# Dense down's weight sums on VectorE, and the experts' up and gate products wide then narrow over two quarters at a time

## The reference, cut to what matters

```python
def _swiglu(h, w_gate, w_up, w_down):
    return (jax.nn.silu(h @ w_gate) * (h @ w_up)) @ w_down

def _moe(h, w_router, w_gate, w_up, w_down):
    """Top-2-of-8 SwiGLU experts, softmax over the selected logits, sorted grouped dispatch."""
    ...
    logits = jnp.einsum('td,de->te', xf, w_router, preferred_element_type=F32)
    top_logits, top_idx = lax.top_k(logits, TOP_K)
    gates = jax.nn.softmax(top_logits, axis=-1)
    ...
    hid = jax.nn.silu(lax.ragged_dot(xs, w_gate, group_sizes)) * lax.ragged_dot(xs, w_up, group_sizes)
    ys = lax.ragged_dot(hid, w_down, group_sizes)
    ys = ys * gates.reshape(-1)[order][:, None].astype(ys.dtype)
    out = jnp.zeros_like(xf).at[tok_sorted].add(ys)
    return out.reshape(B, S, D)

def second_block(x, ...):
    ...
    for l in range(DEPTH_2):
        h = _rmsnorm(x, mix_norm[l])
        ...
        x = x + jnp.concatenate([a, r], axis=-1) @ w_out[l]
        h = _rmsnorm(x, ffn_norm[l])
        if l % 2 == 0:
            x = x + _swiglu(h, dense_w_gate[j], dense_w_up[j], dense_w_down[j])
        else:
            x = x + _moe(h, moe_router[j], moe_w_gate[j], moe_w_up[j], moe_w_down[j])
    return _rmsnorm(x, final_norm)
```

## Time and profile before

| what | us |
|---|---|
| median of three runs | 1756.85 (1754.42 to 1758.68) |
| the profiled execution, time | 1754.76 |
| its span in the trace | 1753.0 |
| TensorE busy | 1699.0 (97%) |
| VectorE, ScalarE, POOL busy | 506.8, 298.9, 290.7 |
| dense stage, column blocks and down | about 500 to 733 in the trace |
| experts | about 898 to 1746 |

### The profile page before, as it was taken

How to read it: one execution, slowest core, us unless ns; L and a number is a source line. 1 busy time by engine, 2 the same in 40 slices (tenths; PEclk the granted TensorE clock), 3 DMA queues, 4 the chain that set the end, 5 groups by cost and what they waited for, 6 DMA issues and landing times.

```text
span 1753.0 us, 25352 instructions
## 1 busy us (share of the span) xinstructions
PE 1699.0 (97%) x11012; PEld 830.0 (47%) x11012; DVE 506.8 (29%) x870; ACT 298.9 (17%) x592; POOL 290.7 (17%) x207
## 2 busy tenths in 40 slices
PE   8999999999999998999999999999999999999997
PEld 4586664455644453447544433343443334444332
DVE  3643224243654236366341100110110101102012
ACT  1210222134311010134211111020110201102011
POOL 0210000042457867037000000000000000000000
PEclk9999999999999998999999999999999999999999
DMA  9742116644334353444648999999999999999997
GB/s 328 262 145 98 49 73 183 225 147 145 104 137 151 115 210 112 159 158 148 238 159 350 422 418 426 420 424 421 390 418 419 426 421 420 422 398 389 421 420 293
DMA packets 114017, 484.84 MB, mean 277 GB/s; under 512 B 15828, under 2 KB 24421, under 8 KB 89966
## 3 DMA queue, kind: packets, MB, share of 16 engines
q1 hardware_dynamic: 106544, 466.53, 67.3%
q0 software_dynamic: 3056, 10.88, 1.7%
q10 hardware_dynamic: 4302, 5.75, 1.0%
HBM read 477.08 MB, written 8.15 MB: 277 GB/s over the span
## 4 chain that ended last, share of the span: by engine, by line
PE 86%; DMA 8%; DVE 2%; issue 2%; ACT 1%; SPq 0%; POOL 0%; ACTq 0%; DVEq 0%; POOLq 0%
PE bank L3299 22%; PE bank L1299 18%; PE bank L1311 14%; PE bank L3363 7%; PE bank L3315 7%; PE bank L3373 4%; DMA ring<-in_moe_w_up 3%; DMA ring<-in_moe_w_down 2%; PE bank L550 2%; PE bank L625 2%; PE bank L1322 2%; PE bank L3331 2%; DMA shift_rows<-ring 1%; DMA ring<-shift_rows 1%; PE bank L1931 1%
## 5 line engine op out<-in xcount | busy, mean ns | idle before, releaser
L3299 PE MATMUL bank<-ring,work 128*64 128x512 f32 x1400 | 397.5, 601 | 8.1 <-DMA ring<-in_moe_w_up 7.3
L1299 PE MATMUL bank<-ring,work 128*128 128x512 f32 (+3 forms) x944 | 387.9, 566 | 5.9 <-DVE work L2303 2.8
L1299 PEld LDWEIGHTS bank<-ring,work 128*128 128x128 f32 x944 | 174.1, 191 | 194.3 <-issue 172.2
L3299 PEld LDWEIGHTS bank<-ring,work 128*64 128x64 f32 x1400 | 124.7, 138 | 206.4 <-issue 204.7
L1311 PE MATMUL bank<-ring,work 128*128 128x512 f32 (+1 forms) x458 | 196.5, 583 | 10.5 <-issue 10.5
L3299 PE MATMUL bank<-work 128*64 128x512 f32 x392 | 172.7, 594 | 0.0
L3363 PE MATMUL bank<-ring,work 128*64 128x512 f32 x704 | 156.8, 595 | 4.3 <-DMA ring<-in_moe_w_down 4.3
L1311 PEld LDWEIGHTS bank<-ring,work 128*128 128x128 f32 x458 | 87.3, 192 | 111.0 <-issue 109.4
L3463 POOL DMA_DIRECT2D expert_rows<-work x7 | 3.6, 521 | 764.5 <-DVE work L3526 605.2
L3315 PE MATMUL bank<-ring,work 128*32 128x256 f32 x1736 | 125.4, 380 | 0.0
L3363 PEld LDWEIGHTS bank<-ring,work 128*64 128x64 f32 x704 | 49.6, 137 | 100.5 <-issue 99.5
(11 more groups left out here) (474 smaller groups left out, 1774.9 us busy)
## 6 DMA issues: line engine op xcount, KB each, us to landing
ring<-in_moe_w_down SPq DMA_DIRECT2D x43, 2048.0 KB, 18.3
ring<-in_moe_w_gate SPq DMA_DIRECT2D x26, 2048.0 KB, 20.2
ring<-in_moe_w_up SPq DMA_DIRECT2D x24, 2048.0 KB, 18.6
ring<-in_w_in SPq DMA_DIRECT2D x20, 2048.0 KB, 8.7
ring<-in_moe_w_up SPq DMA_DIRECT2D x25, 1536.0 KB, 10.9
ring<-in_moe_w_gate SPq DMA_DIRECT2D x23, 1536.0 KB, 13.5
work<-in_moe_w_down SPq DMA_DIRECT2D x12, 2048.0 KB, 16.2
work<-in_moe_w_up SPq DMA_DIRECT2D x8, 2048.0 KB, 22.2
```

Source lines behind the costliest of these rows:

```text
L1299: mm = pe.matmul(banks(j)[:, 0:width], x[:, k0 + kt, tt * P:(tt + 1) * P], w[:, kt, c0:c0 + width], start=first and n == 0, stop=last and ...
L3299: mm = pe.matmul(out[rows, :], xgT[:, q * tiles + k, 0:64], w[n][:, k, cols], start=(q == 0 and k == 0), stop=last)
```

## The change

In the dense stage the down product's weight sums of part 0 stay on POOL; those of parts 1 to 5 are issued by VectorE, each after the part's row sums. `turned_last` comes after part 1's weight sums. On TensorE, product `one` no longer waits for the row sums; product `three` does.

In the experts the quarters are taken in groups of two. Before a group TensorE waits for all of its loads (four), and gives all four slots back at its end. The order in a part becomes wide 0, wide 1, narrow 0, narrow 1 | narrow 2, narrow 3, wide 2, wide 3. In the very first part (e = 0) the groups are (0), (1), (2, 3), and the last runs wide, wide, narrow, narrow. Turns follow each of the two wide quarters of part 1; the wide pick comes after the first group, the narrow pick between narrow 3 and wide 2.

```diff
--- before.py
+++ after.py
@@ -2573,6 +2573,26 @@
         w = core.view(chunk)
         return [w[:, tiles, cols] for tiles in (slice(0, n), slice(n, 2 * n)) for cols in (slice(0, BANK), slice(BANK, DM))]
 
+    def sum_weights(eng, i):
+        chunk, _, n = parts[i]
+        b11, b12, b21, b22 = down_blocks(i)
+        one, two, four = (t[:, 0:n, :] for t in down_weights[i])
+        summed = 4 * n_cols + 4 * i
+        core.wait_weights(eng, chunk)
+        eng.wait_ge(*sevens.weights_summed.at(summed))
+        if i < 4:
+            eng.wait_ge(*banks.ready(J["first", n_cols - 2 + i // 2]))
+        else:
+            eng.wait_ge(down_done, i - 3)
+        eng.tensor_tensor(one, b12, b11, ALU.subtract).then_inc(sevens.weights_summed.sem, 1)
+        eng.wait_ge(*sevens.weights_summed.at(summed + 1))
+        eng.tensor_tensor(two, b22, one, ALU.subtract).then_inc(sevens.weights_summed.sem, 1)
+        eng.wait_ge(*sevens.weights_summed.at(summed + 2))
+        eng.tensor_tensor(b12, b22, b12, ALU.subtract).then_inc(sevens.weights_summed.sem, 1)
+        eng.wait_ge(*sevens.weights_summed.at(summed + 3))
+        eng.tensor_tensor(four, b21, two, ALU.subtract).then_inc(sevens.weights_summed.sem, 1)
+        eng.wait_ge(*sevens.weights_summed.at(summed + 4))
+
     @core.block.tensor
     def _(pe):
         def weights(c):
@@ -2645,10 +2665,9 @@
                                        five=(r1, one, 1), six=(r2, two, 2), seven=(r3, t3, 4))[name]
             if name == "one":
                 core.wait_weights(pe, chunk)
+            elif name == "three":
                 pe.wait_ge(*sevens.rows_summed.at(4 + i + 1))
-                if i == 0:
-                    banks.enter(pe, J[name])
-            elif i == 0:
+            if i == 0:
                 banks.enter(pe, J[name])
             if summed:
                 pe.wait_ge(*sevens.weights_summed.at(4 * n_cols + 4 * i + summed))
@@ -2748,23 +2767,7 @@
             pool.wait_ge(*sevens.weights_summed.at(4 * c + 3))
             pool.tensor_tensor(four, gate[:, hi, :], two, ALU.subtract).then_inc(sevens.weights_summed.sem, 1)
             pool.wait_ge(*sevens.weights_summed.at(4 * c + 4))
-        for i, (chunk, _, n) in enumerate(parts):
-            b11, b12, b21, b22 = down_blocks(i)
-            one, two, four = (t[:, 0:n, :] for t in down_weights[i])
-            summed = 4 * n_cols + 4 * i
-            core.wait_weights(pool, chunk)
-            if i < 4:
-                pool.wait_ge(*banks.ready(J["first", n_cols - 2 + i // 2]))
-            else:
-                pool.wait_ge(down_done, i - 3)
-            pool.tensor_tensor(one, b12, b11, ALU.subtract).then_inc(sevens.weights_summed.sem, 1)
-            pool.wait_ge(*sevens.weights_summed.at(summed + 1))
-            pool.tensor_tensor(two, b22, one, ALU.subtract).then_inc(sevens.weights_summed.sem, 1)
-            pool.wait_ge(*sevens.weights_summed.at(summed + 2))
-            pool.tensor_tensor(b12, b22, b12, ALU.subtract).then_inc(sevens.weights_summed.sem, 1)
-            pool.wait_ge(*sevens.weights_summed.at(summed + 3))
-            pool.tensor_tensor(four, b21, two, ALU.subtract).then_inc(sevens.weights_summed.sem, 1)
-            pool.wait_ge(*sevens.weights_summed.at(summed + 4))
+        sum_weights(pool, 0)
 
     @core.block.vector
     def _(dve):
@@ -2853,11 +2856,11 @@
             if c:
                 turned(c - 1)
         for i in range(len(parts)):
-            if i == split:
-                sum_rows(i)
+            sum_rows(i)
+            if i:
+                sum_weights(dve, i)
+            if i + 1 == split:
                 turned_last()
-            else:
-                sum_rows(i)
         for tt in range(NT):
             dve.wait_ge(*lead.rows[tt])
         j, got = done("one")
@@ -3259,32 +3262,36 @@
             chunks = range(PARTS[n][0], sum(PARTS[n]))
             if n == 0:
                 pe.wait_ge(xg_ready, e + 1)
-            for q in range(QUARTERS):
-                i = 2 * (QUARTERS * n + q)
-                landed(e, i)
-                landed(e, i + 1)
-                w = [first_view(core, e, i), first_view(core, e, i + 1)]
-                if e + n + q == 0:
+            groups = [(0,), (1,), (2, 3)] if e + n == 0 else [(0, 1), (2, 3)]
+            for g, qs in enumerate(groups):
+                w = {}
+                for q in qs:
+                    i = 2 * (QUARTERS * n + q)
+                    landed(e, i)
+                    landed(e, i + 1)
+                    w[q] = [first_view(core, e, i), first_view(core, e, i + 1)]
+                if e + n + g == 0:
                     for k, forms in enumerate(((part_wide, part_narrow), (part_narrow, part_wide))):
                         for form in forms:
                             for c in chunks:
-                                form(e, c, w, q, (c - chunks[0]) * BANK, (k,))
+                                form(e, c, w[q], q, (c - chunks[0]) * BANK, (k,))
                         if k == 0:
                             halves_left[0] = 1
                     pending[0] += 2
                     continue
-                for m, form in enumerate((part_wide, part_narrow)[::-1 if q % 2 else 1]):
-                    for c in chunks:
-                        if form is part_wide or NARROW[e]:
-                            form(e, c, w, q, (c - chunks[0]) * BANK)
-                    if n and q < 2 and m == 0:
-                        turn_chunk(e, 2 * q)
-                        turn_chunk(e, 2 * q + 1)
-                pending[0] += 2
-                if n and q == 1 and e + 1 < NE:
+                for m, form in enumerate((part_wide, part_narrow)[::-1 if g % 2 else 1]):
+                    for q in qs:
+                        for c in chunks:
+                            if form is part_wide or NARROW[e]:
+                                form(e, c, w[q], q, (c - chunks[0]) * BANK)
+                        if n and g == 0 and m == 0:
+                            turn_chunk(e, 2 * q)
+                            turn_chunk(e, 2 * q + 1)
+                    if n and g and m == 0 and e + 1 < NE:
+                        pick_narrow(e + 1)
+                pending[0] += 2 * len(qs)
+                if n and g == 0 and e + 1 < NE:
                     pick(e + 1)
-                if n and q == 2 and e + 1 < NE:
-                    pick_narrow(e + 1)
 
         def part_wide(e, c, w, q, first, ks=range(KD // QUARTERS)):
             out, cols, tiles = wide_of(c), slice(first, first + BANK), KD // QUARTERS
```

## The result

| | before | after |
|---|---|---|
| median, us | 1755.63 (1753.63 to 1758.68, 4 runs) | 1811.13 (1808.23 to 1815.77, 4 runs) |
| the profiled execution | 1754.76 | 1808.23 |
| its span | 1753.0 | 1806.4 |
| experts' first matmul to the first matmul of the scatter | 897.84 to 1742.05 | 894.46 to 1795.49 |

A forecast was written before the change was run, and what follows sets the result against it. The expert stage was taken as a stream of loads that TensorE keeps up with. Dense down -2.2 and experts +50.6 on 1754.76 gave 1803.2 us, forecast as 1804; own range 1795 to 1812, eight in ten 1790 to 1813.

The forecast's parts named there:

- Dense down, -2.2: Dense down: the 10.53 us wait goes, VectorE's added sums bring a new 8.3 us wait before product six; -2.2 us.
- The bound of -13: Dense down: the gain if VectorE were never late with its sums, 10.5 + 2.5 us.
- End of part 0 in e = 0, +3.1: Experts, e = 0: block 4 waits for the first wide multiplication, late after narrow matmuls; +3.1 us (0 to 5).
- The start of e = 2: Experts: e = 2 starts 9.0 (later slots) + 10.0 (four loads before the first matmul) later, and by the 3.1.
- The start of e = 5: Experts: e = 5 starts another 9.0 + 10.0 us later, its stream paced by load (3, 17).
- The ledger: Experts: delays from slots given back later and from waiting for four loads, added up at e = 2, e = 5 and the end.
- The end, +9.0: End of experts: the last load of e = 7, paced by (6, 17), comes 9.0 us later, with no four-load cost.
- The clock, +1.5: Waits before e = 2 and e = 5: slow matmuls cost 3.0 us each, against 1.5 and 3.0 before; +1.5.
- Nine slots did not hold: Experts, rival 1: two groups of four fit in nine slots, every load lands in time; 1751.6 us, chance 0.04.
- Half of it: Experts, rival 2: queued loads cover the later slots, only the fourth load counts, twice; 1776 us, chance 0.1.
- VectorE's sums did not fall to POOL's pace: Dense down, rival 3: VectorE's sums run at POOL's pace, +14 in place of -2.2; 1819 us, chance 0.05.
- The groups formed: Experts, rival 4 said they don't: waits or give-backs still go by single quarters; about 1756 us, chance 0.01.

The follow-up runs named there:

- experiment 11: Kernel before's experts with the changed dense stage, VectorE's sums reordered to run ahead of the last turned block's copy and of later weight sums: 1742.6 us, 0.993.
- experiment 12: The changed kernel with groups only in the wide experts (e = 1, 4 and 7), narrow ones by single quarters: 1769.03 us, 1.0087.
- The two parts alone: The changed kernel grouped only in part 0 of each expert, 1801.45 us (1.0251), or only in part 1, 1789.9 us (1.019).
- waits and give-backs alone: The changed kernel with waits by quarters, 1795.36 us (1.0234), or with give-backs by quarters, 1797.3 us (1.0237).
- `half_after`: The changed kernel with most of the experts' weight loads cut to half their columns: 1744.77 us, 0.9936 to the kernel before.

## Why the prediction was right, and where a size was off

- **Right: what bounds the stage.** The expert stage is a stream of loads paced by nine slots. Halved loads took the cost of the experts' half from 58 us to some 8.
- **Dense down, -2.2.** Measured -3.4 in the changed kernel's trace (-3.0 from the stage's own start) and -3.0 in the time. Each step came as written: no wait at the first product, sums of 1.22 us, the wait before product six. It was 7.43 us in place of 8.3, because a part costs VectorE 6.76 us and not 6.95. The bound of -13 was the right one for sums that are never late: experiment 11 has -13.7 in the trace (-13.2 from the stage's own start) and -12.2 in the time.
- **End of part 0 in e = 0, +3.1.** Measured 3.14 in the trace.
- **The start of e = 2.** It went from 1099.07 to 1120.51, +21.4, or +24.8 from the experts' start. Forecast 19.0 + 3.1 = 22.1, so 2.7 were missed here, or 1.2 if all of the clock's 1.5 is put here. The waits before e = 2 and e = 5 were to be 15 to 20 us and were 16.97 and 17.07.
- **The start of e = 5: the mis-sized term.** "e = 5 starts another 9.0 + 10.0 later" was 19.0; measured 343.84 us from e = 2 to e = 5 against 321.29, so 22.55. This is 3.5 of the 5.0 us that the sum missed. Load (3, 17) divides it. From e = 2's start to its issue it is 181.67 us against 171.24, 10.4 more where 9.5 were forecast; the slower clock behind the longer wait is about that (16.64 us for two quarters, 2.8 lost, against 1.5 before). From its issue to e = 5's start it is 162.17 against 150.05, 12.1 more where 10.0 - 0.5 = 9.5 were forecast. There the stream runs at 0.99 and 412 GB/s (1302 to 1464 us above), in place of 1.01 and 422 from 1302 to 1420 us in the kernel before. The step behind it is "from there on the stream is without a gap until the next narrow run": two small gaps stand there, 1.2 us at 1302 and 1.0 in e = 4, and the rest is a slightly lower rate, whose cause stays open. The gaps of experiment 12 are not the reason: in the changed kernel e = 4 has no pause but that one.
- **Where the stream pauses: the sum right, the places not.** The ledger put 9.0 us of pause right before (3, 17). There the trace has 1.2. The pauses of e = 3 are 3.3, 5.2 and 1.2 us, 9.7 together, and the longest stands at the end of part 0, where four slots come back at once; e = 2 has 9.4 in the same three places. TensorE sets the pace in narrow experts, so (3, 17) still went out 9.4 us late. The number was right because it came from TensorE's pace, not because the queue emptied where the prediction said.
- **The end, +9.0.** From the first matmul of e = 5 to the scatter: 331.14 us against 321.69, +9.45. The number is right, the path is not. "The end is the last load of e = 7" held before; in the changed kernel TensorE no longer waits for a down load at all (4.3 us before). Its last wait for a load is at 1754.84, 5.57 us for the fourth load of e = 7's last group, and from there TensorE sets the end. So "no four loads" was wrong, and that the sum came out is in part luck.
- **The form of the ledger.** Adding 9.0 for slots and 10.0 for the fourth load gave nearly the right number, but the terms cannot be taken one by one. The two parts alone cost 48 and 37 and do not add to 58, waits and give-backs alone return 15.8 and 13.8 and together 22.9. What the traces have in common is idle time of the stream, which a delay from either cause brings about and the other then need not.
- **The clock, +1.5: the other mis-sized term.** It was placed at the starts of e = 2 and e = 5: their first two quarters took 16.64 and 15.39 us where 13.88 is full speed, 2.8 and 1.5 lost where 3.0 each were forecast, and 1.5 + 3.0 before: no growth. It came inside the wide experts instead, where waits are new. In e = 4 67 matmuls at 1376.28 took 17.61 us where 13.88 x 67 / 64 = 14.5 is full speed, 3.1 lost; in e = 1 64 matmuls at 1033.24 took 15.65, 1.8 lost; in e = 7 some 1.6 are lost behind 1720.10 and 3.0 at 1754.84 (8.33 us for 24 matmuls that take 5.37 elsewhere). Pieces of the chain of waits:

```profile
1120.51 16.64 PE bank L3306 x64
...
1353.85 22.29 DMA ring<-in_moe_w_up
1376.28 17.61 PE bank L3306 x67
...
1464.35 15.39 PE bank L3306 x64
```

Over the six places the clock cost some 13.7 us in place of 4.5, 9 us more; TensorE's busy time, 1699.0 us before and 1708.1 after with the same 11012 matmul records, says the same. How much of the 9 us the total time holds is not shown: in wide experts the stream is the slower one, and TensorE would have waited for it anyhow. Ahead of e = 2 the granted clock was 0.67, with TensorE busy for 0.54 of 17.00 us, and 0.50 behind it:

```profile
1103.00:1120.00 17.00, 0.54 (x4) 0.00 (x0) 0.69 (x1) 0.58 (x1) 0.54 (x1) 0.67 1.01 423
1120.00:1126.00 6.00, 5.49 (x14) 1.91 (x16) 0.00 (x0) 0.00 (x0) 0.00 (x0) 0.50 1.01 422
```

- **The rivals.** Nine slots did not hold: TensorE waited 17 us, not none. "Half of it" (1776) fell with the pauses of the stream. VectorE's sums did not fall to POOL's pace: 1.22 us. The groups formed.

What stays open: the 5.0 us missed are a balance. The start of e = 2 holds 2.7, the stretch to e = 5 3.5 and the end 0.4; the dense stage gave 1.2 more than forecast (3.4 at the experts' start, against 2.2), and 0.5 of the sum (clock and switches) has to be set against these stretches. The changed kernel's own runs spread over 7.5 us, so none of these small terms is settled by the times; they are read from one trace each. Groups with a tenth or eleventh slot were not tried.

## What to carry to other kernels

Where a stage is paced by loads through a ring of slots, price a reordering by when each slot comes back, and count the loss as idle time of the transfers: the number of loads issued and not landed at each give-back decides, and causes that each empty the queue do not add. That holds for a step that leaves the order of the compute as it was, too: waiting for and giving back four of nine slots at once cost 16 us over three experts, although TensorE did not stop at the moment when the queue ran dry. And when work is moved from one engine to another to end a wait, look at the new engine's longest pause first: here the same sums, put ahead of the copy that VectorE stood still for, turned -3 us into -12.

## What the runs showed of the hardware

- A VectorE sum of 128x256 beside a POOL sum takes 2.44 us, alone 0.43. The large 128x1024 sum, which stood at 2.35 to 2.41 us on POOL, takes 1.22 on VectorE, so moving it doubled its speed and also freed the smaller sums.
- The clock after the same short wait differed from kernel to kernel. The experts' first 16 matmuls took 3.65 us in the kernel before and 5.35 in `half_after`, behind the same wait of 0.8 us, with a granted clock of 1.00 and 0.72 from 894 to 900 us. The stretch in `half_after`:

```profile
894.00:900.00 6.00, 5.21 (x22) 2.00 (x24) 4.80 (x23) 1.00 (x1) 0.00 (x0) 0.72 0.01 3
```
